# Tail of a fused encoder kernel: who adds tile 1's first choice and tile 3's residual rows

## What is computed

```
h   = layer_norm(ALPHA * x + mix)
ffn = sum over the two experts chosen for a token of  weight * expert(h)      # 16 experts
ple = sigmoid(h @ w_ple_gate) * (p @ w_ple_proj)
x   = layer_norm(ALPHA * h + ffn + ple)                                       # output, 512 x 1024
```

## Time and profile before

| | |
|---|---|
| median of 3 runs | 454.68 us (454.51 to 454.87) |
| profiled execution, its own time | 453.85 us |
| span of its profile, first to last instruction | 452.0 us |
| granted TensorE clock, mean | 0.99 |
| busy: PE / DVE / ACT / POOL | 432.6 / 343.0 / 231.8 / 119.0 us |
| DVE's add of tile 0's first choice | 427.69 to 428.91 us |
| DVE's first `combine` starts | 430.60 us |
| DVE's last write ends | 449.53 us |

### The profile page before, as it was taken

The page is one execution under the profiler, slowest core; times in us unless marked ns, Lnnn a source line. Parts: engine busy times, 40 slices in busy tenths (PEclk is TensorE's granted clock), DMA queues, the critical chain, the costliest instruction groups (busy, mean ns, idle before and its releaser), DMA issues.

```text
span 452.0 us, 5545 instructions
## 1 busy us (share of the span) xinstructions
PE 432.6 (96%) x1983; PEld 307.4 (68%) x1983; DVE 343.0 (76%) x531; ACT 231.8 (51%) x371; POOL 119.0 (26%) x146
## 2 busy tenths in 40 slices
PE   8899999999899999999999999999999999999991
PEld 4667764487566556677687877777777777777661
DVE  3899967987646989998487165778878777779677
ACT  3641433152867850215113155788877777879522
POOL 5800289191039500000007420222212222211200
PEclk9999999999989999999999999999999999999997
DMA  8994104134993971111940149999999999750593
GB/s 267 387 372 129 46 14 97 44 97 129 381 425 119 353 267 48 46 46 48 404 157 1 15 151 424 404 419 421 416 387 384 350 371 383 318 213 21 207 229 139
DMA packets 37210, 103.16 MB, mean 228 GB/s; under 512 B 16060, under 2 KB 22124, under 8 KB 30528
## 3 DMA queue, kind: packets, MB, share of 16 engines
q1 hardware_dynamic: 27888, 91.68, 53.8%
q0 software_dynamic: 5600, 9.44, 6.7%
q10 hardware_dynamic: 3696, 1.71, 1.4%
HBM read 95.39 MB, written 17.86 MB: 251 GB/s over the span
## 4 chain that ended last, share of the span: by engine, by line
PE 81%; DVE 5%; DMA 5%; ACT 5%; SPq 2%; issue 1%; DVEq 0%; POOLq 0%; ACTq 0%
PE bank L1372 8%; PE bank L1175 6%; PE bank L976 6%; PE bank L1344 5%; PE bank L1186 5%; PE bank L1349 4%; PE bank L1353 4%; PE bank L1357 4%; PE bank L1024 4%; DMA region_b<-in_ssm_par 3%; PE bank L1259 3%; PE bank L1260 3%; PE bank L1261 3%; PE bank L1328 3%; PE bank L1016 2%; PE bank L1033 2%
## 5 line engine op out<-in xcount | busy, mean ns | idle before, releaser
L1349 PE MATMUL bank<-gate_up_upper,tokens_upper 128*128 128x512 f32 x96 | 36.2, 459 | 0.0
L1175 PE MATMUL bank<-region_b,region_e 128*128 128x512 f32 x68 | 32.9, 607 | 0.0
L585 POOL DMA_INDIRECT slot_scratch<-region_h,slot_i x8 | 8.9, 1118 | 87.1 <-issue 87.1
L598 POOL DMA_INDIRECT expert_scratch<-region_g,region_h x8 | 10.0, 1254 | 80.1 <-ACT region_g L923 80.1
L1926 DVE TENSOR_TENSOR gate_up_lower<-region_a,gate_up_upper 128x1024 fp32r<-128x1024 f32 x24 | 28.0, 1221 | 3.4 <-ACT gate_up_upper L896 3.4
L1353 PE MATMUL bank<-gate_up_upper,tokens_lower 128*128 128x512 f32 x96 | 29.8, 392 | 0.0
L976 PE MATMUL bank<-region_e,region_a 128*128 128x512 f32 x64 | 28.0, 595 | 0.0
L1259 PE MATMUL bank<-ple_gate_upper,hidden_upper 128*128 128x512 f32 x64 | 25.7, 401 | 0.0
L896 ACT ACTIVATE gate_up_upper<-region_a 128x1024 fp32r<-128x1024 f32 x24 | 23.7, 1057 | 3.2 <-DMA region_a<-in_w_exp_down 3.2
L1349 PEld LDWEIGHTS bank<-gate_up_upper,tokens_upper 128*128 128x128 f32 x96 | 18.1, 189 | 10.4 <-issue 6.2
L1261 PE MATMUL bank<-ple_gate_upper,hidden_lower 128*128 128x512 f32 x64 | 24.9, 390 | 0.0
(11 more groups left out here) (385 smaller groups left out, 1149.1 us busy)
## 6 DMA issues: line engine op xcount, KB each, us to landing
region_a<-in_w_exp_gate SPq DMA_DIRECT2D x8, 1024.0 KB
region_a<-in_w_exp_up SPq DMA_DIRECT2D x8, 1024.0 KB
region_a<-in_w_exp_down SPq DMA_DIRECT2D x8, 1024.0 KB
region_a<-in_w_in SPq DMA_DIRECT2D x3, 1536.0 KB, 13.6
region_b<-in_w_out SPq DMA_DIRECT2D x1, 4096.0 KB, 14.2
expert_scratch<-zero_scratch SPq DMA_DIRECT2D x8, 512.0 KB, 9.7
region_b<-in_w_exp_gate SPq DMA_DIRECT2D x4, 1024.0 KB
region_b<-in_w_exp_up SPq DMA_DIRECT2D x4, 1024.0 KB
```

Of the source, the lines that this page charges most:

```text
L1175: last = mm(bank[WO_AT[half][group]][:], hdT[:, k, t * P:(t + 1) * P], w_o[:, k, half * 512:half * 512 + 512], start=(i == 0), stop=(i == ...
L1349: mm(out_, x_hi[r][:, k * P:(k + 1) * P], w_hi[:, k], start=False, stop=False)
```

## The change

Three edits that belong together.

1. Tile 1's first choice is no longer added by PE's two identity products (L1474) but by DVE, which waits for `y_in1` and adds `y_one[:, 1]` to `xh[:, 1]` right behind the same add for tile 0. `one_added` is now 2, and DVE's wait for it, ahead of the overflow read, too (POOL's wait in its own overflow branch likewise, which this data does not enter).
2. Tile 3's rows of `xh` are added by PE: after `second_choice(3)` it waits for `y_in3` and multiplies the two halves of `xh[:, 3]` by the identity; both late experts follow. The bank then holds the whole sum.
3. `combine(3)` on DVE is gone. ACT, after `deviation(2)`, waits for PE, copies the two halves of the bank to `xh[:, 3]` with a row sum each (`last_sum`); DVE only makes the mean (`last_mean`), and does `scale(2)` ahead of it.

```diff
 # gpsimd, overflow branch
-                gp.wait_ge(S["one_added"], 1)
+                gp.wait_ge(S["one_added"], 2)
 # scalar
             a.preload_act_table(ACT.Sqrt)
-            for t in range(NT):
+            for t in range(NT - 1):
                 deviation(t)
+            ac.wait_ge(S["pe_dn"], NE + 1 + NT)
+            for half in range(2):
+                a.activation(xh[:, NT - 1, half * 512:half * 512 + 512], bank[OH_BANKS[NT - 1][half]][:], ACT.Copy,
+                             accum_out=ln_st[:, NT - 1, half:half + 1]).then_inc(S["last_sum"], 1)
+            deviation(NT - 1)
 # tensor, overflow branch
+                pe.wait_ge(S["o_acc"], 16 * NT * 4)
 # tensor
-            second_choice(1, False)
-            for half in range(2):
-                last = mm(bank[OH_BANKS[1][half]][:], ident[:], y_one[:, 1, half * 512:half * 512 + 512], start=False, stop=True)
-            last.then_inc(S["pe_dn"], 1)
+            second_choice(1, False, True).then_inc(S["pe_dn"], 1)
             both_halves(2, 0, True, False)
             both_halves(2, 1, False, False)
             second_choice(2, False, True).then_inc(S["pe_dn"], 1)
             second_choice(3, True)
+            pe.wait_ge(S["y_in3"], 16)
+            for half in range(2):
+                mm(bank[OH_BANKS[3][half]][:], ident[:], xh[:, 3, half * 512:half * 512 + 512], start=False, stop=False)
             both_halves(3, 0, False, False)
             both_halves(3, 1, False, True).then_inc(S["pe_dn"], 1)
 # vector
             tt(xh[:, 0, :], xh[:, 0, :], y_one[:, 0, :], ALU.add).then_inc(S["one_added"], 1)
-            dv.wait_ge(S["one_added"], 1)
+            dv.wait_ge(S["y_in1"], 32)
+            tt(xh[:, 1, :], xh[:, 1, :], y_one[:, 1, :], ALU.add).then_inc(S["one_added"], 1)
+            dv.wait_ge(S["one_added"], 2)
             n_over = dv.value_load(over_i[0:1, 0:1], min_val=0, max_val=OVER)
...
+            def last_mean():
+                t = NT - 1
+                dv.wait_ge(S["last_sum"], 2)
+                ts(ln_mv[:, t, 0:1], ln_st[:, t, 0:1], ln_st[:, t, 1:2], -1.0 / D, ALU.add, ALU.mult).then_inc(S["z2_ready"], 1)
...
             combine(2)
             centre(2)
-            combine(3)
             scale(2)
+            last_mean()
             centre(3)
             scale(3)
```

More of the change, by code:

```diff
@@ L318, in trunk @@
             "o_vec o_in o_hg o_act o_pe o_out o_round aT_hi dn_hi_set dn_lo_set "
-            "y_in0 y_in1 y_in2 y_in3 o_acc z2_ready one_added pt_moved o_dve out_st").split()}
+            "y_in0 y_in1 y_in2 y_in3 o_acc z2_ready one_added pt_moved o_dve last_sum out_st").split()}
         block = ctx.enter_context(nc.Block())
```

## The result

| | before | changed |
|---|---|---|
| median, 22 executions each | 453.35 us (451.95 to 455.36) | 454.08 us (453.29 to 456.6) |
| profiled execution, own time / span | 453.85 / 452.0 us | 454.11 / 452.3 us |

The ratio is 1.0032 (95% interval 1.0019 to 1.0046), which is 1.45 us slower; the two medians of the table differ by only 0.73 us, and the means of the same executions by 1.09. So the changed kernel is slower, as forecast, and the size of the step (+1.4 us, 0.31% was forecast) is known no better than that. Of the 2.02 us, 1.33 are the reference: the kernel before had a median of 453.35 and not the 454.68 of its first three runs. The other 0.69 is the step as the medians give it, 0.73 and not 1.4.

What follows compares the result with a forecast made beforehand. DVE was taken as the bound from 435.78 us on, after PE's products. The terms +2.35 - 0.4 - 0.9 + 0.35 = +1.4 us, added to the 454.68 median, gave 456.1 us, range 455.1 to 457.0.

Steps and rivals of the forecast that it cites:

- First combine, +2.35: On DVE, combine(0) starts 2.35 us late: 1.22 for the add, 1.15 for the read, branch and restart.
- the no-change rival: On DVE, the overflow read runs during the add: combine(0) 1.3 us late, end +0.35, 455.0; chance 11 in 100.
- The 0.4 given back at combine(1): On DVE, combine(1) no longer waits for PE, which has tile 1 early: a gain of 0.4 us.
- Edit 3 gives back 0.9, loses 0.35: At tile 3, the missing combine(3) gains 0.9 us; deviation(3), now starting with centre(3), delays scale(3) by 0.35.
- the bound that the prediction gave for it: At last_mean, if ACT's copies were faster than 1.6 us, DVE at 447.3 would be the limit, a gain of 0.1.
- PE's wait for y_in3: Before tile 3's identity products PE stalls 0.6 to 0.7 us, at no cost as long as ACT comes later.
- The cover: PE is done with tile 3 at about 443.7, ACT's copies start at 445.8: a cover of 2.1 us.
- the third rival: PE's tail becomes the bound if `y_in3` lands over 2.1 us later than 439.8; 1.5 further gives 457.6; chance 5 in 100.
- The sum: Against the profiled execution, the whole change adds +2.35 - 0.4 - 0.9 + 0.35 = +1.4 us.
- The step that failed: For the whole kernel's median: 454.68, the reference, plus 1.4 gives 456.1 us, slower by 0.31%.
- the range: For the whole kernel's median, 455.1 to 457.0 us: read hidden at the low end, branch's 0.5 and copies' 0.4 at the high.

Runs made afterwards that it cites:

- e13: The changed kernel timed once more, with nothing altered, against the kernel before: ratio 1.0026 (1.0009 to 1.0043).
- e3: The changed kernel with DVE's overflow read moved ahead of its wait for `y_in1`; against the kernel before, ratio 1.0021 (1.0002 to 1.0040).
- e7: The kernel before with POOL instead of PE adding tile 1's first choice, tile 3 as before; against the kernel before, ratio 0.9992 (0.9971 to 1.0012).
- e6: The changed kernel with POOL instead of DVE adding tile 1's first choice, edits 2 and 3 kept; against the kernel before, ratio 1.0023 (1.0006 to 1.0040).
- e9: The changed kernel with the overflow read ahead of the wait and tile 1's first choice loaded before its second; against the kernel before, ratio 1.0053 (1.0031 to 1.0075).
- e4: The kernel before plus a DVE wait for `y_in1` ahead of the overflow read, without the add; against the kernel before, ratio 0.9998 (0.9978 to 1.0019).
- e1: The changed kernel without edit 1, so edits 2 and 3 alone; against the kernel before, ratio 1.0006 (0.9981 to 1.0030).
- e2: The kernel before with edit 1 alone, tile 3 as before; against the kernel before, ratio 1.0033 (1.0015 to 1.0051).
- e8: The kernel before timed against itself, with no change: ratio 0.9999 (0.9983 to 1.0015).
- e5: The changed kernel with tile 1's first choice loaded ahead of its second, on its own semaphore; against the kernel before, ratio 1.0050 (1.0027 to 1.0073).
- e12: The changed kernel with DVE's overflow read done twice in a row; against the kernel before, ratio 1.0033 (1.0014 to 1.0052).

## Why the prediction was right in its step and wrong in its time

**First combine, +2.35.** Measured +2.10 from the tail's start in the profile after (+2.19 in e13). The parts: the load landed 0.3 earlier against the tail's start (6.59 us after issue, not 7.1), the add 1.22 as taken, and from the add's end to combine(0) 1.28 where I had 1.15: the branch's restart is 0.24 (431.77 to 432.01), not ACT's 0.1. The landing differs from execution to execution: the forecast had the add at 3.53, the six profiles have 3.16 to 3.74. The two misses pull in opposite directions, so the sum is nearer than its parts. That the read is exposed is shown by e3, which takes 0.93 us off by moving it; the no-change rival, a read that runs beside the add, is refuted by the chain.

By the Trainium skill (Runtime: NRT & Kernel Launch, section Instruction fetch mechanics) a taken branch whose target lies outside the instructions already fetched has to wait until they are fetched. Behind the branch in the profile after, the 0.16 us of issue is all the room that there is for such a wait; whether the target had already been fetched is not shown.

**The 0.4 given back at combine(1).** Measured 2.10 - 1.71 = 0.39, and shown by itself in e7 (-0.40 at combine(1)).

**Edit 3 gives back 0.9, loses 0.35.** Measured 1.00 (1.71 to 0.71) and 0.35 (0.71 to 1.06). The copies were mis-sized: 1.25 us for two, not 1.6. The first step is 0.57 us where the row has 0.72, the second copy with its read 0.68 and not 0.82, and there is no 0.1 for a semaphore. So DVE and not ACT set the last mean, the bound that the prediction gave for it.

**PE's wait for y_in3.** 0.81 us, covered by 1.4, in the profile after: right there. The cover was forecast at 2.1; it is thinner, and in e13 it was 0.36. So the third rival, put at 5 in 100, was nearer than I said; no profile of the changed kernel shows it, and the timed runs don't exclude it for some executions. e6 and e9 show what is behind it.

**The sum.** +1.4 forecast. In the profile after the terms are +2.10 - 0.39 - 1.00 + 0.35 = +1.06; e13 has +1.14. Timed it is +1.45 (0.9 to 2.1) and +1.2 (0.4 to 1.9) by the ratios, +0.73 and +1.13 by the medians. The mechanism was right, the size somewhat high.

**The step that failed** is the last one, put as "the median of the runs shown is 0.83 above the profiled time; the forecast for the median is 454.68 + 1.4 = 456.1", and with it the range: all of its width was for the costs of the edits, and none for the reference. Three executions within 0.4 us of each other were taken for the kernel's level; 22 of them span 3.4 us with a median 1.33 lower, and later sets were lower still. The profiled execution, at 453.85, already stood lower than all three, and I passed over it.

One place where such differences can arise is in the records. Shortly before 125 us PE waits 2.0 us for DVE in all 17 profiles. The ten products right behind that wait, and the window behind it (columns as in e6), in the kernel before:

```profile
124.73 2.05 PE L1081 MATMUL bank<-ident,region_a 128*128 128x128 f32 x10 [1.96 <-DVE region_a L1701]
```
```profile
125.00:128.50 3.50, 3.50 (x14) 2.47 (x13) 3.19 (x7) 3.47 (x6) 0.00 (x0) 0.52 1.04 419
```

and in e4:

```profile
124.36 1.38 PE L1081 MATMUL bank<-ident,region_a 128*128 128x128 f32 x10 [1.96 <-DVE region_a L1701]
```
```profile
125.00:128.50 3.50, 3.50 (x16) 2.31 (x17) 3.00 (x7) 3.47 (x6) 0.00 (x0) 1.00 1.03 411
```

The same wait, but in one execution the granted clock was 0.52 over this window, near 1.2 GHz, and the ten products took 2.05 us; in the other it was 1.00, 2.4 GHz, and they took 1.38. The window is at 0.52 to 0.68 in seven of the 17 profiles (before, changed, e1, e2, e7, e8, e9) and at 1.00 in ten; the tail's start has a median of 426.33 in the seven and 425.37 in the ten. Over the 22 executions of the changed kernel, the 7 with a mean clock of 0.994 or more have a median of 453.45 us, the other 15 of 454.73. That goes together; that the clock makes the whole difference was not tested.

## What to carry to other kernels

An idle engine is not free room: ask what its sequencer does in the gap. Here 1.69 us of idle DVE time looked like space for a 1.22 us add, but the add's operand landed at its very end, and behind it stood a 1.05 us register read and branch that the busy columns don't count.

A wait that is covered today (PE's for tile 3) is covered by somebody's delay; before removing that delay, price the wait again, and with the latest landing seen and not with one profile's. And if the step is 0.3%, forecast the ratio: take the reference from every execution at hand, and give the level a width of its own.

## What the hardware showed that I had not expected

- The same one-word register read on DVE took 0.55 us in most profiles, 0.61 in e4, 1.38 in e5, and 0.32 when it was repeated at once (e12).
- A ScalarE copy of 128x512 from PSUM with a row sum steps by 0.57 us beside its own duration of 0.58: the accumulator read overlaps the next copy, and the last one ends 0.10 us behind its copy, so that two copies take 1.25 us.
- The granted clock after a PE pause of 2.0 us fell to half in seven of 17 profiles and stayed at 1.00 in ten (the windows above); in e6 it stretched the kernel's last products from 0.39 to 0.63 us each.
- Of the two accumulating loads of 512 KB the first landed 9.1 to 11.3 us after its issue and the second 11.0 to 13.7, over all 17 profiles.
